# High and low half of a rounded weight pair 4352 instead of 4224 bytes apart, in a two-block transformer kernel

## The reference

```
for l in range(DEPTH):                       # DEPTH = 2
    h = rms_norm(x, norm1[l])
    proj = h @ w_in[l]
    ...                                      # four attentions on parts of proj
    x = x + mixed @ w_out[l]
    h2 = rms_norm(x, norm2[l])
    x = x + jnp.square(jax.nn.relu(h2 @ w_up[l])) @ w_down[l]
...
proj = h @ w_in_2[l]                         # the second block
y_a = y_a @ w_proj_a[l]
y_b = y_b @ w_proj_b[l]
x = x + gate[:, None] * (merged @ w_out_2[l])
```

## Time and profile before

| | |
|---|---|
| median of three runs | 2161.43 us |
| lowest, highest | 2159.44, 2162.81 us |
| span of the profiled execution, first to last instruction | 2157.7 us |
| TensorE busy | 2067.6 us (96%) |
| VectorE busy | 1122.1 us (52%) |
| ScalarE busy | 836.3 us (39%) |
| mean granted TensorE clock, as a share of full speed | 0.989 |

### The profile page before, as it was taken

How to read it: one execution, slowest core, us unless ns; L and a number is a source line. 1 busy time by engine, 2 the same in 40 slices (tenths; PEclk the granted TensorE clock), 3 DMA queues, 4 the chain that set the end, 5 groups by cost and what they waited for, 6 DMA issues and landing times. The chain is left out here.

```text
span 2157.7 us, 28306 instructions
## 1 busy us (share of the span) xinstructions
PE 2067.6 (96%) x10898; PEld 1685.8 (78%) x10902; DVE 1122.1 (52%) x1971; ACT 836.3 (39%) x1732; POOL 199.1 (9%) x169
## 2 busy tenths in 40 slices
PE   8999999999999999999999999799999999999997
PEld 7777777888887877777888887688787887777776
DVE  5787534423434498744552543578674333225545
ACT  4354633312323244643331332453433336324532
POOL 1331000000000143001000000002031330000100
PEclk9999999999999999999999999999999999999999
DMA  6321022232333432002542433223234223331232
GB/s 184 93 84 40 1 69 88 88 108 82 95 117 77 116 96 81 2 30 79 184 158 97 165 118 109 87 81 91 76 79 135 75 64 115 109 98 31 78 118 78
DMA packets 177527, 198.33 MB, mean 92 GB/s; under 512 B 38755, under 2 KB 140786, under 8 KB 176882
## 3 DMA queue, kind: packets, MB, share of 16 engines
q1 hardware_dynamic: 177394, 196.53, 29.6%
HBM read 180.74 MB, written 11.55 MB: 89 GB/s over the span
## 5 line engine op out<-in xcount | busy, mean ns | idle before, releaser
L160 DVE TENSOR_TENSOR weight_pairs<-weight_ring,weight_pairs 128x1024 fp32r<-128x1024 f32 (+4 forms) x293 | 355.7, 1217 | 446.7 <-ACT weight_pairs L151 446.0
L181 PE MATMUL psum<-operand,weight_pairs 128*128 128x512 f32 x1320 | 527.5, 400 | 18.8 <-PEq L203 13.9
L151 ACT ACTIVATE weight_pairs<-weight_ring 128x1024 fp32r<-128x1024 f32 (+4 forms) x293 | 303.4, 1038 | 577.7 <-PE psum L183 546.5
L183 PE MATMUL psum<-operand,weight_pairs 128*128 128x512 f32 x1320 | 527.1, 399 | 0.0
L182 PE MATMUL psum<-operand,weight_pairs 128*128 128x512 f32 x1320 | 525.9, 398 | 0.0
L181 PEld LDWEIGHTS psum<-operand,weight_pairs 128*128 128x128 f32 x1320 | 254.1, 192 | 84.4 <-issue 22.6
L182 PEld LDWEIGHTS psum<-operand,weight_pairs 128*128 128x128 f32 x1320 | 249.5, 189 | 55.1 <-issue 1.0
L183 PEld LDWEIGHTS psum<-operand,weight_pairs 128*128 128x128 f32 x1320 | 249.3, 189 | 54.0
L182 PE MATMUL psum<-weight_pairs,hidden 128*128 128x512 f32 x512 | 202.2, 395 | 0.0
L181 PE MATMUL psum<-weight_pairs,hidden 128*128 128x512 f32 x512 | 200.5, 392 | 0.0
L183 PE MATMUL psum<-weight_pairs,hidden 128*128 128x512 f32 x512 | 199.2, 389 | 0.0
(11 more groups left out here) (419 smaller groups left out, 2767.2 us busy)
## 6 DMA issues: line engine op xcount, KB each, us to landing
weight_ring<-in_w_in_dram SPq DMA_DIRECT2D x100, 512.0 KB, 3.6
weight_ring<-in_w_up_dram SPq DMA_DIRECT2D x64, 512.0 KB, 3.7
weight_ring<-in_w_down_dram SPq DMA_DIRECT2D x64, 512.0 KB, 3.5
weight_ring<-in_w_out_dram SPq DMA_DIRECT2D x24, 512.0 KB, 3.5
ada_rows<-in_ada_w_dram SPq DMA_DIRECT2D x24, 512.0 KB, 4.6
spilled<-v_t SPq DMA_DIRECT2D x22, 256.0 KB, 4.3
weight_ring<-in_w_in_dram SPq DMA_DIRECT2D x20, 256.0 KB, 2.9
weight_ring<-in_w_proj_a_dram SPq DMA_DIRECT2D x8, 512.0 KB, 3.4
```

The lines of the kernel that those rows point to most:

```text
L151: act.activation(self.pairs[:, i % SPLIT_RING, 0, 0:n], self.buf[:, i % RING, 0:n], ACT.Copy).then_inc(self.rounded, 1)
L160: dve.tensor_tensor(self.pairs[:, i % SPLIT_RING, 1, 0:n], self.buf[:, i % RING, 0:n], self.pairs[:, i % SPLIT_RING, 0, 0:n].bitcast(F32), ...
L181: pe.matmul(out, lhs[0], rhs[0], start=start, stop=False)
L183: return pe.matmul(out, lhs[1], rhs[0], start=False, stop=stop)
```

## The change

The width of a half's place in `weight_pairs` becomes 1088 float32 numbers instead of 1056, so the low half begins 4352 bytes behind the high half instead of 4224, and a slot takes 8704 bytes instead of 8448. The items, the number of elements that each instruction handles, the ring, the order and the waits are as before. The tensor grows by 768 bytes in each partition, and every tensor behind it begins 768 bytes later.

```
@@ -74,6 +74,7 @@
 RING = 4
 SPLIT_RING = 3
 SLOT = 1056
+PAIR_SLOT = 1088
 
@@ -103,7 +104,7 @@
 
     def __init__(self, nc, ctx):
         self.buf = ctx.enter_context(nc.sbuf_tensor("weight_ring", [P, RING, SLOT], F32))
-        self.pairs = ctx.enter_context(nc.sbuf_tensor("weight_pairs", [P, SPLIT_RING, 2, SLOT], F32R))
+        self.pairs = ctx.enter_context(nc.sbuf_tensor("weight_pairs", [P, SPLIT_RING, 2, PAIR_SLOT], F32R))
```

## The result

The changed kernel takes 2143.27 us (median of four, 2141.94 to 2144.82) against 2162.12 us for the kernel before: a ratio of 0.9912, 95% interval 0.9898 to 0.9926. That is 19 us less, where I had forecast no change with 91% and a range down to 2156 us. It was timed a second time beside later experiments and gave 0.9912 again (0.9897 to 0.9928).

The account below looks back on a forecast made before the run. TensorE's stream of matmuls was taken to bound the kernel. All parts were priced at 0, so the forecast stayed at the earlier median, 2161.4 us, with a range of 2156 to 2167 us.

Parts of the forecast that it names:

- The reading of the bound: Whole kernel: TensorE's stream of matmuls sets the time, with some 18 ns of each matmul not explained by its columns.
- (a) on TensorE: Matmuls with weight pairs: high-to-low distance going from 4224 to 4352 bytes changes the pace by 0.
- The sharper row: Ten triples, eight loading 16 columns instead of 128, run at 0.689 us, so the load does not take the 18 ns.
- Step (b): Matmuls on the three pair slots: slot distance going from 8448 to 8704 bytes changes TensorE's pace by 0.
- The bounds: TensorE's triples: all at the fastest kind's 0.687 us, 12.6 us less; all at the slowest's 0.700, 15.3 us more.
- Rival 1: Matmul pace: leftover is a clash between the halves that the new distance ends; likelier form 2149 us, full prize 2048; 3%.
- Steps (a) on VectorE and ScalarE: Splits of weight pairs: the new distance changes their times by 0; at worst five doubled splits, 6 us more.
- (c): Tensors behind the pairs start 768 bytes later: 0, with bounds of 12.6 us less and 15.3 us more.
- The rule weighed: Matmul gap: skill's 215.8 ns against the trace's 231 would make 98 us a stall layout might free; discounted.

Follow-up runs that it names:

- the last experiment: Changed kernel with blocks of 420 and 16 columns set 448 and 64 elements apart and latent_t moved 32 bytes: 2140.20 us, against the changed kernel's 2142.96 us.

## Why the prediction was wrong

**The reading of the bound held.** TensorE's pace sets the time, and the idea that 18 ns a matmul "are what an address could be guilty of" was right in part: 5 to 7 ns were, in two of three matmuls by channels and one of three by tokens with hidden.

**The step that failed is (a) on TensorE.** It took 0 for the pace. Measured were 0.681 and 0.680 us a triple in place of 0.694, 0.687 and 0.700. I compared the distance inside one tensor with the distance inside another (4224 streamed against 2048 streamed) and found that the pace did not follow it. That was true, and the wrong pair of things. What counts is the relation between the streamed and the loaded tensor. The numbers were at hand: operand begins at 49792 + 3 x 8448 = 75136, so the activations' halves are 128 past a multiple of 256, the weights' high half too, the low half on one. I wrote that down as a relation between high and low only, and said that operand and hidden "have been in phase all along", without asking in phase with what. Had I tabulated, for each of the three products, streamed start against loaded start, the second and third matmul's 396 and 397 ns beside the first's 389 would have stood out: the earlier trace rows shows 0.23 us for each, rounded over just the 6 ns in question.

**The sharper row was no test.** The triples with 16-column loads take their columns from blocks that begin 64 bytes apart, so they run through the phases 0, 64, 128 and 192 whichever way the halves lie. Before, the first of the eight started at 1393.25 and the last at 1398.12 us: 4.87 / 7 = 0.696 us a triple; my 0.689 had two triples with full loads in it, over starts rounded to 0.1 us. After the change they take what they took:

```profile
L182 PE MATMUL psum<-operand,weight_pairs x10: 391/394/398, 1382.3 to 1388.6; 128*16 128x512 f32 x8, 128*128 128x512 f32 x2
```

6.3 / 9 = 0.70 us. Nor are the phases what holds them back: with all eight in phase they took 0.696 again (the last experiment). So narrow loads run at a pace of their own, for a reason that no run here shows, and it is by chance that this pace lay beside that of the full loads before. I took the two equal numbers as proof that the load does not matter.

**Step (b) tested only what is harmless.** The slots differ by 8448 = 33 x 256 bytes, and hidden lies 26112 = 102 x 256 bytes further on in the second layer. Both are moves by whole multiples of 256, so that they left the pace alone said nothing about moves by half of one. (8448 is an odd multiple: the first product of a triple by channels took 227.1 ns on the mean whether the two starts were equal modulo 512 or 256 apart, so 256 is enough.)

**The bounds were too narrow below.** I let the fastest kind of the trace, 0.687 us, be the floor, and got 12.6 us. All kinds had a product out of phase, so none showed the true floor of 0.680. With it the sum is (1312 + 112) x 0.013 + 512 x 0.007 + 128 x 0.020 + 64 x 0.007 = 25.1 us; of the 192 that I had at 0.700, the 64 of the second block's output projection ran at 0.687. Rival 1, with 3% and 2149 us, had the sign and the place, an address as the cause of the leftover. Its mechanism, a clash between the halves that the new distance ends, is T2, and that fell.

**Steps (a) on VectorE and ScalarE, and (c), held.** 1225 against 1226 ns, 1060 against 1060; the rest moved alone gave 0.9994.

**Why 19 and not 25 us.** Part comes from stages that other engines pace: the 520 triples of the second block's projections should give 6.8 us and take 510.2 instead of 514.5 us from first to last start, 4.3 less. Part is clock. In the profiled execution, which gained 14.6 us in span, the granted clock after the change is lower in three stretches. (The spans differ by less than the medians, since the execution profiled before was by its span the shortest of four and the one after the longest.) Before (busy us of PE, PEld, DVE, ACT, POOL, then the clock and DMA):

```profile
175.00:280.00 105.00, 99.06 (x786) 76.19 (x787) 63.28 (x200) 61.96 (x206) 0.00 (x0) 1.00 0.03 11
852.00:957.00 105.00, 98.27 (x781) 75.37 (x781) 62.59 (x199) 61.95 (x205) 0.00 (x0) 1.00 0.03 11
...
1990.00:2110.00 120.00, 113.71 (x555) 88.62 (x554) 65.66 (x124) 52.75 (x103) 8.98 (x6) 0.97 0.28 97
```

After:

```profile
175.00:280.00 105.00, 99.06 (x774) 76.29 (x774) 61.97 (x198) 61.90 (x206) 0.00 (x0) 0.98 0.03 11
852.00:957.00 105.00, 100.64 (x736) 75.84 (x739) 60.66 (x191) 60.23 (x199) 0.00 (x0) 0.97 0.03 9
1990.00:2110.00 120.00, 115.07 (x493) 90.96 (x494) 58.00 (x74) 42.82 (x55) 8.54 (x6) 0.94 0.30 106
```

From the end of the front's products to the output projection the first two stretches cost 1.5 and 2.5 us more than before. In the kernel with everything 128 bytes later, they cost nothing more, yet its span was 2142.7 us, hardly less, because stretches in its first 120 us ran slower. Whether a faster stream brings these dips on, or they fall where they will, no experiment here separates; that stays open.

**The rule weighed.** The Trainium skill's figure of N / 2.4 + 2.5 ns for isolated warm matmuls (TensorE: Matmul & The Clock Gate, Back-to-back issue gap) would be 215.8 ns. The best measured here is 226.7. The stall above the figure was partly layout, as I allowed with 3%, and 11 ns of it are still unexplained. The sentence by which I discounted this, that TensorE's port never waits on anyone (SBUF — State Buffer, SBUF: two separate sides), may be right between engines; in these runs TensorE's pace follows how its own two reads lie to each other. By what means is not shown.

## What to carry to other kernels

Where float32r matmuls stream 512 columns and load 128, put every tensor that is streamed and every tensor that is loaded with it at the same place modulo 256 bytes: pad halves and slots to multiples of 64 elements, and start the tensors alike. For narrower streams or loads, measure first: here 420 columns ran no faster in phase, and loads of 16 columns stayed as they were. To judge a layout, tabulate streamed start minus loaded start for each matmul instruction, not distances within one tensor. A row that does not change when something is varied proves nothing until one has checked that it was not in the bad state already; and the fastest row of a trace is no floor if all rows share the fault.

## What the runs showed of the hardware that I had not expected

- Where all products of a triple have streamed and loaded tensor 4 bytes apart modulo 256, a 512-wide float32r matmul costs 232 (loaded 4 bytes further on) to 237 ns (streamed 4 bytes further on) from start to start instead of 226.9. Of 14 phases measured 0 is the fastest, the next best 192 with 229.3 and 229.5.
- Where only some products are out of phase, the costs do not add up: 0.687 us by tokens with two of three at phase 128, and 0.687 or 0.700, by the stage, with one.
- In phase, the three products of all kinds with 512-wide streams and loads of 128 columns run at the same 0.680 us. That is 544 steps of the 2.4 GHz clock per matmul for 512 columns.
- The cost is in the relation alone: moving both operands by 128 bytes left 0.9913, and 4352 or 13056 bytes between the halves gave 0.9912 and 0.9899.
- 420-wide products gain nothing from it: 193.4 ns in phase, 192.2 with half the blocks out of phase, 190.9 before. Loads of 16 columns take 0.696 us a triple with all in phase, as with phases 0, 64, 128 and 192.
